# First norm's rows read from DMA instead of row products, and the experts' places put in a written order with one place more

## The chip, the cores and the metric

One NeuronCore of one Trainium2 chip runs the whole program. The metric is the device time of one execution in microseconds (us). The kernel before takes 1349.5 us, the median of 3 runs (1349.09 to 1349.57).

## The reference

Input `x` is 256 tokens by 1024. Everything is float32. Four layers follow each other; each is a mixer and then a mixture of experts.

```
h = layer_norm(x, ln0_g, ln0_b)
for i in 0, 1:                         # layers 0 and 1 of the kernel
    u   = h @ w_in[i]                  # 1024 x 2560; hyena, differential attention, pooling
    h   = layer_norm(a*h + concat(mixers(u)) @ w_out[i], ...)
    h   = layer_norm(a*h + moe16(h) + sigmoid(h @ ple_wg + b) * (p @ ple_wp), ...)
for i in 0, 1:                         # layers 2 (gmlp) and 3 (mla) of the kernel
    x   = x + concat(mixer_i(rms_norm(x)), memory_attention) @ w_out
    x   = x + moe32(rms_norm(x), ...)
# moe16: 4 groups x 4 experts; moe32: 4 groups x 8 experts; each token picks 2 experts of one group
# an expert: (silu(t @ w_gate) * (t @ w_up) * weight) @ w_down, with 1024x256, 1024x256, 256x1024 matrices
```

An expert has three matrices of 1 MiB each. The 32 experts of layer 2, and those of layer 3, are 96 MiB a layer and all of it is read once from HBM.

## The kernel before

**Dense part.** A weight matrix comes in units of 128 x 2048 numbers (1 MiB, two DMAs) into 4 raw slots of SBUF, issued by SP (line 585). ACT copies each half of a unit into `w_hi` (L1960, a rounded form), DVE subtracts it into `w_lo` (L2575), and PE does three products for one (L973 to L975). Activations are transposed on PE (L990) and split in the same way by ACT into `t_hi` (L1966) and by DVE into `t_lo` (L2587). `w_hi` and `w_lo` have 3 parts each.

**First norm.** SP loads `x` (L746), then one row of gains and one of biases, 4 KB each, into partition 0 (L748), then the first `w_in` units. Four PE products of a column of ones with a half row (`first_row`, L1447) spread the rows over 128 partitions in PSUM banks 0 to 3. DVE's `first_norm` (L3216) waits for them one after the other: `shift` (L2631) and `scale` (L2637) of the first half of the channels, `h_a`, then of the second half, `h_b`. The small constants come by a DMA that POOL issues.

**Experts of layers 2 and 3** (`slot_experts`). The work goes in steps of 4 experts (`ST_` = 4): 8 steps here. A step uses 12 transfers of 1 MiB in this order: 4 gates, 4 ups, 4 downs. I number the transfers of a layer from 0; group g is the transfers 4g to 4g+3, so groups 0, 1, 2 are gate, up and down of step 0, group 3 the gates of step 1, and so on. PE does gate and up with L1343 (64 products a group) and down with L1360 (32 products). Step 0 runs: the first gather of tokens (L1303, L1304, after DVE's `sel`), gate, `rows` (L1323 to L1326), up, `turn_glu` (L1351), down, then the second gather (16 products of each kind of 512 columns), and step 1 begins.

A transfer needs a place of 8 KB on each partition. The places are what the dense part leaves: 4 raw slots and 3 parts of `w_hi` and of `w_lo` (a0 to a9 in what follows), one that was `y` (OWN, a10), the region of `t_hi`/`t_lo` (FIRST_TOKENS, TOKENS, MORE_TOKENS: the gathered tokens take it back later), ROWS (the gain rows' buffer), SPARE, LATER, and in layer 3 MEMORY. The class `Ring` (L105) makes the list `units`, the place of each transfer: 12 of step 0, 12 of step 1, then `fixed` for all later steps. A transfer into a place that was used before waits on SP until the PE products that read it have counted up `used` (`ring.before`); a transfer into a fresh place waits for what the dense part had there (L714 to L733). SP issues in order (`ring.issued`), so a transfer that waits holds up all behind it. Fresh places: 16 in layer 2, 17 in layer 3. The list before, layer 2, with groups separated by bars:

```
step 0: ROWS SPARE LATER a0 | a1 a2 a3 a4 | a5 TOKENS MORE_TOKENS a6
step 1: a7 a8 a9 a10 | a0 a1 a2 a3 | a4 a5 a6 a7
later:  a8 a9 a10 a0 | a1 a2 a3 FIRST_TOKENS | a4 a5 a6 a7
layer 3, step 0: MEMORY ROWS SPARE LATER | a0 a1 a2 a3 | a4 a5 TOKENS MORE_TOKENS
layer 3, step 1: a6 a7 a8 a9 | a10 a0 a1 a2 | a3 a4 a5 a6
```

**Experts of layers 0 and 1** (`pair_experts`, `PairRing`). Steps of 2 experts with 6 transfers (2 gates, 2 ups, 2 downs; L642 and L646 issue them, L1123 and L1140 use them). The first two transfers go to the places SUMS and MEMORY, which come free before the ring's own places.

**DVE's selection** (`pick`, L3072): for each of two blocks of 128 tokens a `tensor_scalar` and a `scalar_tensor_tensor` write the gather's selection matrix; each waits for the one before it. It is used once for the first gather (`sel`), once for the second (`sel2`), and in the last steps (`select`).

Of the kernel before, what the change touches and what calls it, by code (L numbers as in the profile page):

```python
# [95 lines left out]
SUMS = LATER + 1  # L96
# [8 lines left out]
class Ring:  # L105


    MAIN = 6

    def __init__(self, unit, more, by_release):  # L110
# [9 lines left out]
        self.more = more  # L120
        first = more + a[0:6] + [TOKENS, MORE_TOKENS] + a[6:n]
        self.units = first + (a + a)[n:n + 12] + self.fixed * (self.MAIN - 2)
        fresh, release = range(13 + len(more)), by_release(a)
        self.issued = sorted(fresh, key=lambda i: release.index(self.units[i])) + [*range(len(fresh), self.MAIN * self.per)]

    def landed(self, n):
        for together in (self.more, [TOKENS, MORE_TOKENS]):
            if self.units[n] in together:
                return 16 * len(together)
        return 16 * self.units[0:n + 1].count(self.units[n])  # L130
# [20 lines left out]
class PairRing:  # L151
# [4 lines left out]
    def __init__(self, unit):  # L156
# [4 lines left out]
        self.units = [SUMS, MEMORY] + [r[n % 10] for n in range(self.main - 2)]  # L161
# [80 lines left out]
def program(nc, A, seen):  # L242

    ctx = ExitStack()
    with ctx:
# [117 lines left out]
        def place(slot):  # L363
            return {MEMORY: MEMW, SPARE: SPAREW, LATER: LATERW, SUMS: SUMSW}[slot] if slot > ROWS else EX[:, slot, :]

# [150 lines left out]
        class SlotSignals:  # L516
            def __init__(self, L):
# [32 lines left out]

        def ring_of(L, s):
            m = slot_signals[L]
            if m.ring is None:
                if L < DEPTH:
                    m.ring = PairRing(s.unit)
                elif L == 2:
                    m.ring = Ring(s.unit, [ROWS, SPARE, LATER], lambda a: [ROWS, OWN, SPARE, a[0], LATER] + a[1:10] +
                                  [TOKENS, MORE_TOKENS])
                else:
                    m.ring = Ring(s.unit, [MEMORY, ROWS, SPARE, LATER], lambda a: [MEMORY, a[0], a[1], OWN, a[2], ROWS, SPARE, LATER] +  # L560
                                  a[3:10] + [TOKENS, MORE_TOKENS])
# [12 lines left out]
        def _(sp):  # L574
# [61 lines left out]
            def load_pairs(L):  # L636
# [11 lines left out]
                n = 0  # L648
                for step in range(ring.STEPS):
                    for k in range(4 if step == 0 else 6):  # L650
                        slot, before = ring.units[n], ring.before(n)
                        if before is not None:
                            sp.wait_ge(m.used, before + 1)
                        elif slot in (SUMS, MEMORY):
                            sp.wait_ge(*turn_lo.at((("cat", L), 1)))
                        elif slot < RING:
                            sp.wait_ge(split_half[1], s.count(last_dense(s.unit, slot) + 1 - s.unit))
                        else:
                            sp.wait_ge(unit_used, s.count(last_dense(s.unit, slot) + 1 - s.unit))
                        if k < 4:  # L660
# [3211 lines left out]
```

## Time and profile before

| | |
|---|---|
| median of 3 runs | 1349.5 us |
| the profiled execution, its own time | 1349.16 us |
| span of its trace (first to last instruction) | 1345.9 us |
| PE busy | 1153.6 us (86%) |
| DVE busy | 704.4 us (52%) |
| ACT busy | 464.8 us (35%) |
| moved by DMA | 399.58 MB, mean 297 GB/s |

The profile page gives, for one execution, how long each engine was busy and what moved in 40 equal slices of the span. The chain that ended last is followed back from the last instruction to what released each step of it. Busy shares are averages over stages with different limits, so the stages have to be read one by one: where an engine waits, for whom, and whether DMA is moving data at that time. Between the profiled time and the span lie 3.3 us of start and end.

### The profile page before, as it was taken

What the parts mean: (1) busy time and instruction counts of PE and PEld (TensorE: products, weight loads), DVE (VectorE), ACT (ScalarE), POOL (GpSimd) and SP (SyncE); (2) the same over time, 40 slices, a digit from 0 to 9 for tenths busy, and PEclk for the clock granted to TensorE, in tenths of its full rate; (3) what the DMA queues carried; (4) which work ended last, traced back from release to release, by engine and by line L of the source; (5) the groups of instructions that cost most, each with busy time, mean ns of one, the idle gap of its engine ahead of it and who ended that gap; (6) DMA issues with size and microseconds to landing.
All of it is one profiled execution on the core that took longest, in us unless ns stands there. A gap on an engine that the chain in (4) does not pass through costs nothing.

```text
span 1345.9 us, 20019 instructions
## 1 busy us (share of the span) xinstructions
PE 1153.6 (86%) x7730; PEld 807.1 (60%) x7730; DVE 704.4 (52%) x1530; ACT 464.8 (35%) x863; POOL 166.3 (12%) x264
## 2 busy tenths in 40 slices
PE   7999999979999999989998966667799988755675
PEld 4888775547987765567876532334489775422342
DVE  6787854348778844376755521102477766211022
ACT  3574521125555322146743300000378643000010
POOL 4012200022030900011004000000222120000000
PEclk9999999989999999989998987878999998877888
DMA  9445489987346699975469699999843396899996
GB/s 329 150 157 173 159 356 422 390 320 233 126 136 234 224 404 420 401 260 168 159 227 373 235 414 421 421 420 422 333 168 125 126 373 270 354 421 421 421 420 287
DMA packets 94156, 399.58 MB, mean 297 GB/s; under 512 B 12124, under 2 KB 20060, under 8 KB 56948
## 3 DMA queue, kind: packets, MB, share of 16 engines
q1 hardware_dynamic: 84708, 381.98, 72.7%
q0 software_dynamic: 9360, 16.40, 3.9%
q8 instruction: 58, 0.95, 0.3%
q14 instruction: 30, 0.25, 0.1%
HBM read 397.29 MB, written 1.05 MB: 296 GB/s over the span
## 4 chain that ended last, share of the span: by engine, by line
PE 58%; DMA 23%; DVE 13%; ACT 4%; issue 2%; SPq 1%; DVEq 0%; ACTq 0%; POOLq 0%
DMA experts_at<-in_moe_w_down_dram 12%; DMA experts_at<-in_moe_w_up_dram 8%; PE bank L973 8%; PE bank L974 8%; PE bank L975 7%; PE bank L1123 7%; PE bank L1343 4%; PE bank L1360 4%; PE bank L1140 4%; DVE w_lo_at L2575 2%; PE bank L1150 2%; PE bank L990 1%; DMA experts_at<-in_moe_w_dram 1%; PE bank L1460 1%; PE bank L1303 1%
## 5 line engine op out<-in xcount | busy, mean ns | idle before, releaser
L973 PE MATMUL bank<-w_hi_at,t_hi_at 128*128 128x512 f32 (+3 forms) x528 | 209.7, 397 | 11.7 <-DVE t_lo_at L2597 4.1
L974 PE MATMUL bank<-w_lo_at,t_hi_at 128*128 128x512 f32 (+3 forms) x528 | 202.5, 383 | 0.0
L975 PE MATMUL bank<-w_hi_at,t_lo_at 128*128 128x512 f32 (+3 forms) x528 | 202.4, 383 | 0.0
L2575 DVE TENSOR_TENSOR w_lo_at<-raw_at,w_hi_at 128x1024 fp32r<-128x1024 f32 (+2 forms) x152 | 176.3, 1203 | 21.8 <-ACT w_hi_at L1960 16.3
L1960 ACT ACTIVATE w_hi_at<-raw_at 128x1024 fp32r<-128x1024 f32 (+2 forms) x152 | 148.8, 1035 | 35.0 <-PE bank L975 23.6
L1343 PE MATMUL bank<-experts_at,xs_at 128*32 128x256 f32 x1456 | 110.0, 454 | 51.4 <-DMA experts_at<-in_moe_w_gate_dram 32.7
L973 PEld LDWEIGHTS bank<-w_hi_at,t_hi_at 128*128 128x128 f32 x528 | 101.1, 192 | 36.0 <-issue 8.8
L1343 PEld LDWEIGHTS bank<-experts_at,xs_at 128*32 128x32 f32 x1456 | 61.7, 130 | 99.5 <-issue 82.6
L975 PEld LDWEIGHTS bank<-w_hi_at,t_lo_at 128*128 128x128 f32 x528 | 101.2, 192 | 18.9
L3153 DVE SCALAR_TENSOR_TENSOR glu_at<-silu_at,gate_at,bank 128x256 f32<-128x256 f32 x16 | 10.5, 657 | 194.7 <-ACT silu_at L2140 194.7
L974 PEld LDWEIGHTS bank<-w_lo_at,t_hi_at 128*128 128x128 f32 x528 | 101.4, 192 | 16.9 <-issue 0.5
L1360 PE MATMUL bank<-experts_at,act_t_at 128*32 128x512 f32 x512 | 78.6, 769 | 37.7 <-DMA experts_at<-in_moe_w_down_dram 35.3
L1123 PE MATMUL bank<-experts_at,xs_f_at 128*64 128x256 f32 x960 | 108.4, 380 | 0.0
L1123 PEld LDWEIGHTS bank<-experts_at,xs_f_at 128*64 128x64 f32 x960 | 69.5, 137 | 38.5 <-issue 8.6
L2140 ACT ACTIVATE silu_at<-bank,root_slot_at 128x256 f32<-128x256 f32 x16 | 7.6, 474 | 233.2 <-PE bank L1343 233.2
L3162 DVE TENSOR_TENSOR ys_lo_at<-bank,ys_hi_at 128x512 fp32r<-128x512 f32 x32 | 22.1, 691 | 106.0 <-ACT ys_hi_at L2153 105.9
L1360 PEld LDWEIGHTS bank<-experts_at,act_t_at 128*32 128x32 f32 x512 | 21.7, 136 | 85.9 <-issue 85.9
L1140 PE MATMUL bank<-experts_at,act_t_at 128*64 128x512 f32 x256 | 58.0, 595 | 0.2 <-DMA experts_at<-in_moe_w_dram 0.2
L2153 ACT ACTIVATE ys_hi_at<-bank 128x512 fp32r<-128x512 f32 x32 | 19.1, 598 | 108.9 <-PE bank L1360 108.9
L1343 PE MATMUL bank<-experts_at,xs_loop_at 128*32 128x256 f32 x512 | 40.0, 474 | 18.0 <-DMA experts_at<-in_moe_w_up_dram 12.4
L1343 PEld LDWEIGHTS bank<-experts_at,xs_loop_at 128*32 128x32 f32 x512 | 18.8, 135 | 36.7 <-issue 14.5
L2912 DVE TENSOR_TENSOR ys_lo_at<-bank,ys_hi_at 128x512 fp32r<-128x512 f32 x32 | 22.1, 691 | 34.9 <-ACT ys_hi_at L2047 34.5
(656 smaller groups left out, 2042.4 us busy)
## 6 DMA issues: line engine op xcount, KB each, us to landing
experts_at<-in_moe_w_dram SPq DMA_DIRECT2D x92, 1024.0 KB, 11.0
experts_at<-in_moe_w_up_dram SPq DMA_DIRECT2D x64, 1024.0 KB, 18.6
experts_at<-in_moe_w_down_dram SPq DMA_DIRECT2D x64, 1024.0 KB, 18.8
experts_at<-in_moe_w_gate_dram SPq DMA_DIRECT2D x59, 1024.0 KB, 18.1
raw_at<-in_w_in_dram SPq DMA_DIRECT2D x40, 512.0 KB, 6.3
raw_at<-in_a_w_in_dram SPq DMA_DIRECT2D x20, 512.0 KB, 4.6
raw_at<-in_w_out_dram SPq DMA_DIRECT2D x16, 512.0 KB, 4.2
raw_at<-in_ple_wg_dram SPq DMA_DIRECT2D x16, 512.0 KB, 5.1
```

The costliest lines, as they stand in the source:

```text
L973: pe.matmul(out, ah, bh, start=start, stop=False, skip_group_check=loose)
L974: pe.matmul(out, ah, bl, start=False, stop=False, skip_group_check=loose)
L975: return pe.matmul(out, al, bh, start=False, stop=stop, skip_group_check=loose)
L1123: ins = pe.matmul(out[C * t:C * t + C], x[:, j, off + C * t:off + C * t + C], w, start=first and n == 0, stop=last and n == len(chunks) - ...
L1140: ins = pe.matmul(BK[4 + half][C * t:C * t + C, :], ATF[:, i, C * t:C * t + C], place(slots[t])[:, a:a + 512], start=i == 0, stop=i == 1, ...
L1150: ins = pe.matmul(BK[2 * tb + half][:, :], st[:, tb * P:(tb + 1) * P], y[:, half * 512:half * 512 + 512], start=first and y is YHF, stop=F ...
L1343: ins = pe.matmul(out[C * t:C * t + C], x[:, j, off + C * t:off + C * t + C], w, start=first and n == 0, stop=last and n == len(chunks) - ...
L1360: ins = pe.matmul(BK[4 + half][C * t:C * t + C, :], ATT[:, i, C * t:C * t + C], place(slots[t])[:, a:a + 512], start=i == 0, stop=i == 1, ...
L1960: act.activation(WH[:, s.part(), a], RAW[:, s.slot(), a], ACT.Copy).then_inc(hi_half[i], 1)
L2575: dve.tensor_tensor(WL[:, s.part(), a], RAW[:, s.slot(), a], WH[:, s.part(), a].bitcast(F32), ALU.subtract).then_inc(split_half[i], 1)
L2912: dve.tensor_tensor(YLF[:, a], BK[4 + half][:, :], YHF[:, a].bitcast(F32), ALU.subtract)\
L3162: dve.tensor_tensor(YL2[:, a], BK[4 + half][:, :], YH2[:, a].bitcast(F32), ALU.subtract)\
```

## The change

- The two rows of the first norm are loaded by SP's DMA into all 128 partitions (512 KB each where 4 KB were), in front of the first `w_in` units. The four `first_row` products are gone; two products of 512 columns on constants stand on PE after the wait for the constants. DVE waits for both rows at once.
- `Ring` takes a plan: the lists of places for step 0, step 1 and later steps are written out for each layer. There is one place more, SUMS2, in the 8 KB where `x_t` lay (free when the router's logits are done), so 17 fresh places in layer 2 and 18 in layer 3. FIRST_TOKENS isn't used any more; SPARE (layer 2) and MEMORY (layer 3) stay in the later steps. `diag2` moves to another address. Which landing semaphores are shared changes with it.
- `PairRing` keeps its order of issue, but the transfers to SUMS and MEMORY are now the two ups of step 0, and the gates go to the ring's first two places.
- POOL loads the memory tokens of layer 1 after 4 uses rather than 2, and layer 3's gain rows (into ROWS) after 9 uses rather than 1.
- `pick` does the first operation for both blocks, one wait, the second for both, one wait; PE waits for one `sel` signal rather than two.

```
step 0, layer 2: SPARE LATER a0 a1 | a2 a3 a4 SUMS2 | ROWS TOKENS MORE_TOKENS a5
step 1, layer 2: a6 a7 a8 a9 | a10 SPARE a0 a1 | a2 a3 a4 a5          later: the same
step 0, layer 3: MEMORY SPARE LATER a0 | ROWS a1 a2 SUMS2 | a3 a4 TOKENS MORE_TOKENS
step 1, layer 3: a5 a6 a7 a8 | a9 a10 MEMORY SPARE | a0 ROWS a1 a2
later,  layer 3: a3 a4 a5 a6 | a7 a8 a9 a10 | MEMORY a0 a1 a2
```

```diff
-    def __init__(self, unit, more, by_release):
+    def __init__(self, unit, plan):
...
-        n = 10 - len(more)
-        b = (a + a)[n + 1:n + 12]
-        self.fixed = b[0:7] + [FIRST_TOKENS] + b[7:11]
+        first, second, self.fixed, release, self.together = plan(a)
...
-        first = more + a[0:6] + [TOKENS, MORE_TOKENS] + a[6:n]
-        self.units = first + (a + a)[n:n + 12] + self.fixed * (self.MAIN - 2)
-        fresh, release = range(13 + len(more)), by_release(a)
+        self.units = first + second + self.fixed * (self.MAIN - 2)
+        fresh = range(len(release))
...
-        self.units = [SUMS, MEMORY] + [r[n % 10] for n in range(self.main - 2)]
+        self.units = r[0:2] + [SUMS, MEMORY] + [r[n % 10] for n in range(2, self.main - 2)]
+        self.issued = [2, 3, 0, 1] + [*range(4, self.main)]
...
-        DG2, XT = sb("diag2", [P, 10, P], z.at), sb("x_t", [P, DC, T], z.at)
+        XT, SUMS2W = sb("x_t", [P, DC, T], z.at), sb("sums_place2", [P, UNIT], z.at)
         YH2, YL2 = (z.take(n, [P, D], F32R) for n in ("ys_hi2", "ys_lo2"))
         SEL = z.take("sel2", [P, TB, 512], F32R)
+        DG2 = sb("diag2", [P, 10, P], z.at)
...
+        def gmlp_places(a):
+            turns = a[6:11] + [SPARE] + a[0:6]
+            return ([SPARE, LATER] + a[0:5] + [SUMS2, ROWS, TOKENS, MORE_TOKENS, a[5]], turns, turns,
+                    [ROWS, OWN, SPARE, a[0], LATER] + a[1:10] + [TOKENS, MORE_TOKENS, SUMS2], (ROWS, TOKENS, MORE_TOKENS))
+
+        def mla_places(a):
+            return ([MEMORY, SPARE, LATER, a[0], ROWS, a[1], a[2], SUMS2, a[3], a[4], TOKENS, MORE_TOKENS],
+                    a[5:11] + [MEMORY, SPARE, a[0], ROWS, a[1], a[2]], a[3:11] + [MEMORY] + a[0:3],
+                    [MEMORY, a[0], a[1], OWN, a[2], ROWS, SPARE, LATER] + a[3:10] + [TOKENS, MORE_TOKENS, SUMS2],
+                    (TOKENS, MORE_TOKENS))
...
+                    elif slot == SUMS2:
+                        sp.wait_ge(*small_ready.at(("logits_t", L)))
...
-                    elif slot == FIRST_TOKENS:
-                        sp.wait_ge(m.used, per + 2 * G)
...
-                sp.dma_start(ROW[0:1, slot, :], A[n].rearrange("(a n) -> a n", a=1)).then_inc(*first_rows.tick("ln0"))
+                sp.dma_start(ROW[:, slot, :], A[n].partition_broadcast(P)).then_inc(*first_rows.tick("ln0"))
...
-                    pool.wait_ge(slot_signals[L].used, 2)
+                    pool.wait_ge(slot_signals[L].used, 4)
...
-                        (A["b_kn_g_2"][0][P:192], 0, 832)], (slot_signals[2].used, 1))
+                        (A["b_kn_g_2"][0][P:192], 0, 832)], (slot_signals[2].used, 9))
...
-            pe.wait_ge(*first_rows.at("ln0"))
-
-            def first_row(half, slot):
-                pe.matmul(BK[2 * half + slot][:, :], ONES[0:1, :], ROW[0:1, slot, 512 * half:512 * half + 512],
-                          start=True, stop=True).then_inc(*small_ready.tick(("ln0_row", half, slot)))
-            first_row(0, 0)
-            first_row(0, 1)
...
+            for _ in range(2):
+                pe.matmul(BK[7][:, :], IDENT, CS[:, 0:512], start=True, stop=True)
...
-                def pick(c, tb, key, a, ramp, sel=SEL):
-                    c.do(dve.tensor_scalar(sel[:, tb, a], ramp, key[:, 0, tb:tb + 1], None, ALU.is_equal))
-                    c.do(dve.scalar_tensor_tensor(sel[:, tb, a], ramp, key[:, 1, tb:tb + 1], sel[:, tb, a].bitcast(F32),
-                                                  ALU.is_equal, ALU.add))
+                def pick(c, key, a, ramp, sel=SEL):
+                    for tb in range(TB):
+                        c.go(dve.tensor_scalar(sel[:, tb, a], ramp, key[:, 0, tb:tb + 1], None, ALU.is_equal))
+                    c.sync()
+                    for tb in range(TB):
+                        c.go(dve.scalar_tensor_tensor(sel[:, tb, a], ramp, key[:, 1, tb:tb + 1], sel[:, tb, a].bitcast(F32),
+                                                      ALU.is_equal, ALU.add))
+                    c.sync()
...
-                dve.wait_ge(*small_ready.at(("ln0_row", 0, 0)))
-                shift(X, 0, row_in_bank)
+                dve.wait_ge(*first_rows.at("ln0"))
+                shift(X, 0, row_of)
                 rooted("ln0", TB)
-                dve.wait_ge(*small_ready.at(("ln0_row", 0, 1)))
-                scale(X, 0, row_in_bank)
+                scale(X, 0, row_of)
```

## Rows read from the trace of the kernel before

**Rows 1.** The page, its chain that ended last: shares of the span by engine.
```profile
PE 58%; DMA 23%; DVE 13%; ACT 4%; issue 2%; SPq 1%; DVEq 0%; ACTq 0%; POOLq 0%
```

**Rows 2.** By stretch, layers 2 and 3: length, busy per engine, granted PEclk, DMA share, GB/s.
```profile
741.00:747.00 6.00, 6.00 (x85) 4.25 (x84) 5.46 (x23) 2.47 (x6) 0.15 (x1) 1.00 0.00 0
...
769.00:774.00 5.00, 5.00 (x71) 3.10 (x71) 2.88 (x10) 0.00 (x0) 0.00 (x0) 1.00 0.13 16
774.00:958.00 184.00, 121.68 (x1162) 61.48 (x1160) 31.92 (x84) 15.47 (x34) 0.00 (x0) 0.83 1.01 419
...
1121.00:1130.00 9.00, 7.50 (x112) 4.93 (x104) 5.53 (x17) 2.67 (x5) 0.00 (x0) 1.00 0.05 8
...
1146.00:1150.00 4.00, 4.00 (x55) 2.55 (x48) 1.89 (x7) 0.00 (x0) 0.00 (x0) 1.00 0.23 31
1150.00:1334.00 184.00, 121.17 (x1161) 62.18 (x1159) 31.91 (x84) 15.47 (x34) 0.00 (x0) 0.83 1.00 416
```

**Rows 3.** Instructions in time, PE, layer 2: start us, us, what, [idle before, releaser].
```profile
769.07 3.66 PE L1343 MATMUL bank<-experts_at,xs_at 128*32 128x256 f32 x64
...
781.06 3.64 PE L1360 MATMUL bank<-experts_at,act_t_at 128*32 128x512 f32 x32 [0.56 <-ACT act_t_at L2144]
788.97 6.21 PE L1343 MATMUL bank<-experts_at,xs_at 128*32 128x256 f32 x64 [4.27 <-DMA experts_at<-in_moe_w_gate_dram]
```

**Rows 4.** The same view, SP's DMA issues, layer 2.
```profile
746.71 7.17 SPq L697 DMA_DIRECT2D experts_at<-in_moe_w_up_dram  x4
...
772.74 0.33 SPq L701 DMA_DIRECT2D experts_at<-in_moe_w_down_dram  x1
```

**Rows 5.** The same view, SP's DMA issues, layer 3.
```profile
1128.51 0.33 SPq L697 DMA_DIRECT2D experts_at<-in_moe_w_up_dram  x1
...
1148.58 0.33 SPq L701 DMA_DIRECT2D experts_at<-in_moe_w_down_dram  x1
```

**Rows 6.** The same view, PE, layer 3: up of step 0, gate of step 2.
```profile
1124.83 3.66 PE L1343 MATMUL bank<-experts_at,xs_at 128*32 128x256 f32 x64
...
1164.49 1.94 PE L1343 MATMUL bank<-experts_at,xs_at 128*32 128x256 f32 x16 [4.23 <-DMA experts_at<-in_moe_w_gate_dram]
```

**Rows 7.** The same view, DVE, layer 2: a block's selection, and a pair without a wait.
```profile
737.29 0.36 DVE L3073 TENSOR_SCALAR sel_at<-ramp_at,keys_at 128x256 fp32r<-128x256 f32 x1 [0.18 <-DVE sel_at L3074]
...
744.69 0.28 DVE L3109 TENSOR_SCALAR diag_at<-consts_at,w_at 128x128 f32<-128x128 f32 x1
744.88 0.48 DVE L3111 TENSOR_SCALAR diag_at<-consts_at,rs_at 128x128 f32<-128x128 f32 x2
```

**Rows 8.** The same view, the first 18 us, four engines' rows.
```profile
9.24 1.41 DVE L2631 SCALAR_TENSOR_TENSOR x_at<-x_at,mv_at,bank 128x512 f32<-128x512 f32 x2 [1.78 <-PE bank L1447]
...
11.11 2.01 ACT L1960 ACTIVATE w_hi_at<-raw_at 128x1024 fp32r<-128x1024 f32 x2 [3.36 <-DMA raw_at<-in_w_in_dram]
...
13.70 0.60 ACT L1966 ACTIVATE t_hi_at<-bank 128x512 fp32r<-128x512 f32 x1 [0.58 <-PE bank L990]
...
15.12 1.28 DVE L2587 TENSOR_TENSOR t_lo_at<-bank,t_hi_at 128x512 fp32r<-128x512 f32 x2
...
17.49 0.79 PE L973 MATMUL bank<-w_hi_at,t_hi_at 128*128 128x512 f32 x1
```

**Rows 9.** Layer 0: SP's issue in time, and a stretch (columns as Rows 2).
```profile
183.24 0.82 SPq L642 DMA_DIRECT2D experts_at<-in_moe_w_dram  x2
...
196.00:200.00 4.00, 4.00 (x37) 2.50 (x36) 2.27 (x6) 0.47 (x2) 0.00 (x0) 1.00 0.15 64
```

**Rows 10.** In time: layer 3's first loads, and ACT's use of their second and third unit.
```profile
945.40 11.63 SPq L585 DMA_DIRECT2D raw_at<-in_b_w_in_dram  x8
...
968.14 3.28 ACT L1960 ACTIVATE w_hi_at<-raw_at 128x640 fp32r<-128x640 f32 x4
```

**Rows 11.** In time: POOL's loads of memory tokens (layer 1) and of gain rows (layer 2).
```profile
469.84 1.06 POOL L783 DMA_DIRECT2D mem_at<-in_mem_dram  x2
...
746.85 0.54 POOL L772 DMA_DIRECT2D row_at<-in_b_kv_norm_g_dram  x1 [7.75 <-PE bank L1343]
```

More of the change, by code:

```diff
@@ L95 @@
 FIRST_TOKENS, TOKENS, MORE_TOKENS, ROWS, MEMORY, SPARE, LATER = OWN + 1, OWN + 2, OWN + 3, OWN + 4, OWN + 5, OWN + 6, OWN + 7
-SUMS = LATER + 1
+SUMS, SUMS2 = LATER + 1, LATER + 2
 def last_dense(unit, slot):
@@ L363, in place @@
         def place(slot):
-            return {MEMORY: MEMW, SPARE: SPAREW, LATER: LATERW, SUMS: SUMSW}[slot] if slot > ROWS else EX[:, slot, :]
+            return {MEMORY: MEMW, SPARE: SPAREW, LATER: LATERW, SUMS: SUMSW, SUMS2: SUMS2W}[slot] if slot > ROWS else EX[:, slot, :]
         z = Space(z_at, z_size)
@@ L523, in __init__ @@
                 else:
-                    once = {slot: "once" if slot >= ROWS else "tokens" for slot in range(TOKENS, LATER + 1)}
-                    self.land = [sem(f"s{L}_land_{once.get(slot, slot)}") for slot in range(LATER + 1)]
+                    self.land = {}
                 self.used = sem(f"s{L}_used")
@@ L553, in ring_of @@
             if m.ring is None:
[L554 to L561, printed above, removed]
+                m.ring = PairRing(s.unit) if L < DEPTH else Ring(s.unit, gmlp_places if L == 2 else mla_places)
+                if L >= DEPTH:
+                    for slot in m.ring.units:
+                        name = "together" if slot in m.ring.together else slot
+                        m.land[slot] = sem(f"s{L}_land_{name}")
             assert m.ring.unit == s.unit, (L, m.ring.unit, s.unit)
@@ L646, in down @@
                     sp.dma_start(place(slot)[:, :], src).then_inc(m.land[ring.pair[slot]], 16)
[L648 to L660, printed above, removed]
-                            up(slot, 2 * step + k % 2, k // 2)
-                        else:
-                            down(slot, 2 * step - 2 + k % 2)
-                        n += 1
+                steps = [(0, k) for k in range(4)] + [(step, k) for step in range(1, ring.STEPS) for k in range(6)]
+                for n in ring.issued:
+                    step, k = steps[n]
+                    slot, before = ring.units[n], ring.before(n)
+                    if before is not None:
+                        sp.wait_ge(m.used, before + 1)
+                    elif slot in (SUMS, MEMORY):
+                        sp.wait_ge(*turn_lo.at((("cat", L), 1)))
+                    elif slot < RING:
+                        sp.wait_ge(split_half[1], s.count(last_dense(s.unit, slot) + 1 - s.unit))
+                    else:
+                        sp.wait_ge(unit_used, s.count(last_dense(s.unit, slot) + 1 - s.unit))
+                    if k < 4:
+                        up(slot, 2 * step + k % 2, k // 2)
+                    else:
+                        down(slot, 2 * step - 2 + k % 2)
                 sp.wait_ge(*dve_ready.at(("table", L)))
@@ L1314, in slot_experts @@
                 pe.wait_ge(*pool_ready.at(("hl", L, 1)))
-                for tb in range(TB):
-                    pe.wait_ge(*dve_ready.at(("sel", L, tb)))
+                pe.wait_ge(*dve_ready.at(("sel", L)))
                 first_gather(range(5))
@@ L2623, in row_of @@
                 return ROW[:, slot, 512 * half:512 * half + 512]
-            def row_in_bank(slot, half):
-                return BK[2 * half + slot][:, :]
             def shift(buf, half, row):
@@ L3114, in slot_experts @@
                 dve.wait_ge(*gathered.at((L, DC - 1)))
-                for tb in range(TB):
-                    pick(ch, tb, KLS, slice(0, 512), RAMP[:, :])
+                pick(ch, KLS, slice(0, 512), RAMP[:, :])
                 done(("sel2", L))
@@ L3120, in select @@
                 def select(c):
-                    for tb in range(TB):
-                        pick(c, tb, KLS, slice(0, P), IOTA, SELL)
+                    pick(c, KLS, slice(0, P), IOTA, SELL)
                     dve.nop().then_inc(*m.sel.tick())
@@ L3232, in first_norm @@
                 sync()
-                dve.wait_ge(*small_ready.at(("ln0_row", 1, 1)))
-                scale(X, 1, row_in_bank)
+                scale(X, 1, row_of)
                 done(("h_b", 0))
```

21 lines of the change are left out of this document (6 added, 15 removed).

## The prediction

> **What bounds the kernel now.** I began with the chain that ended last: PE carries 58% of it, DMA 23%, DVE 13% [rows 1]. The kernel therefore has two kinds of stage, and an edit has to be priced in its own. The table by stretch separates them [rows 2]. In layer 2 from 774 to 958 and in layer 3 from 1150 to 1334 the DMA share is 1.0 at 419 and 416 GB/s, while PE works 122 and 121 of 184 us: there only bytes count. Just ahead of both stretches DMA stands nearly still: 0 GB/s in 741 to 747, 16 in 769 to 774, 8 in 1121 to 1130, 31 in 1146 to 1150, with PE busy nearly throughout. PE, running step 0, sets that time.
>
> Why DMA stands still is read from SP. In layer 2 it issues when a group of PE products has freed places: at 746.71 (end of gate 0) and at 772.74 (end of gate 1, which began at 769.07 and took 3.66) [rows 3, 4]. Layer 3 does the same at 1128.51, the end of up 0, and 1148.58, the end of gate 1 [rows 5, 6]. No place is free in between. Later PE waits: gate 2 begins at 788.97 after 4.27 us of waiting for DMA, in layer 3 at 1164.49 after 4.23 [rows 3, 6].
>
> So the end of each layer is the moment at which transfers stop being held up (after gate 1) plus the transfers left then. One is 1.0486 MB; at 419 GB/s it takes 2.50 us, at 416 2.52. From 774 to 958 that is 184/2.50 = 73.5, and 96 less the 23 moved before is 73: the picture closes. **A transfer moved earlier, into the idle time, is worth 2.5 us.**
>
> **The change part by part.**
>
> *Places.* I counted both lists of places by hand: how many transfers, in order of issue, have a place at the start and after gate 0, up 0, down 0 and gate 1 (later groups in the same way).
>
> Layer 2, before: 16, 17, 21, 23, 27. After: 17, 20, 23, 24, 28.
> Layer 3, before: 17, 17, 21, 23, 27. After: 18, 21, 24, 26, 30.
>
> What counts is the column after down 0, since these can have landed when gate 1 ends. Layer 2 goes from 23 to 24: only the extra place counts. Layer 3 goes from 23 to 26: the extra place, and two that came back late before, because MEMORY and two of its neighbours in step 0 weren't in the later steps or were followed in the list by places freed only by an up or a down.
>
> Is there room? In layer 2, SUMS2 (free with the router's logits, ahead of the first gather) lands inside the idle 741 to 747. The three of 746.7 take 7.5 us and end near 754, the three after up 0 (near 752.5) near 762, the one after down 0 (near 761.6) near 765; the loads for the new row at POOL add about 1 us, and gate 1 ends only at 772.7. In layer 3, the three after gate 0 (near 1123) end near 1131, three after up 0 (1128.5) near 1138.6, two after down 0 near 1143.6; gate 1 ends at 1148.5. All fits, with 5 us or more to spare. Afterwards both rings turn with the same 12 transfers a step, and PE has 62 us of slack in 184, so the lead isn't lost. Gain: 1 x 2.50 in layer 2, 3 x 2.50 = 7.5 in layer 3; together 10.0. Lead above zero can't turn into a loss by itself, but SUMS2 can be late: in layer 3 it is issued a little before 1121 and lands by 1123.6 to 1124, up 0 begins at 1124.83 [rows 6]. The margin is some 0.5 us or more; I take 0, with a bound of 1 us lost.
>
> Against that sum a page can be held: the Trainium skill, DMA: Bandwidth & Descriptors, section Where 436 GB/s comes from, says that for transfers from HBM a core's share of some 358 GB/s binds. By it, as an estimate, a transfer would take 2.93 us and the ten would be 11.7. The trace has 419 and 416 GB/s [rows 2], and the measurement decides.
>
> *Selection.* `pick` stands on the way to the first gather, when DMA is idle, so what it saves moves all of gate 0 to gate 1, the whole rest of the layer with it. Now each of the four operations waits for the one before (0.18 us idle ahead of one [rows 7]). Two waits go. An operation of 128 columns takes 0.28, and two in a row without a wait take 0.48 together, not 0.56 [rows 7]: an overlap of 0.08. Each pair gains 0.18 - 0.04 (the gap that remains, by the nearest such rows) + 0.04 to 0.08, about 0.18; two pairs 0.37, both layers 0.74. `sel2` and `select` get it too, but PE doesn't wait for them. Bounds 0 and 1.0.
>
> The rule against it: the Trainium skill, VectorE: DVE Perf Modes, section The DRAIN you can't avoid, says that dropping semaphores between VectorE operations gains nothing, the next one starts when the pipe is empty either way. By it this term is 0; the trace has the overlap of 0.08 for the pair at 744.88.
>
> *First norm.* The rows bring 1 MB ahead of the first `w_in` unit, 2.50 us at 419 GB/s. Before, `shift` began at 9.24, after 1.78 us of waiting for a row product, and ACT began on the first unit at 11.11, waiting for DMA [rows 8]. After: the rows stand behind `x`, whose statistics DVE has before its wait begins at 7.46; 1.25 us for each of the two puts them near 8.5 (an estimate), so `shift` gains up to 0.7; ACT begins at 11.11 + 2.5 = 13.6, `w_hi` takes 2.01 to 15.6, two `t_hi` of 0.60 to 16.9, and the second `t_lo` (half of 1.28) to 17.5. The first unit's products began at 17.49 [rows 8]: the loss on DMA is met by slack, since `t_hi` waited for PE before (0.58 ahead of 13.70), where row products stood in front of the transposes. I take 0. If ACT's delay counted in full it is +2.6; if the four products in front of the unit were what held it, -1.0.
>
> *Layers 0 and 1.* SP's issue for the gates no longer stands behind SUMS and MEMORY's, which wait for the split at 183.24; but DMA is saturated there until 196 and then idles at 64 GB/s until PE releases places [rows 9]. PE bounds the stage: 0, bounds -0.5 and +0.5.
>
> *Order of the other queues.* Layer 3's first raw units (SP, 945.40 [rows 10]) go into places that the last downs now free, some 5 us later; ACT's need of the second and third unit is at 968.14, and they land near 963.5 and 966: hidden, by 0 to 1 us lost. POOL's memory tokens wait for 4 uses, which are there at about 470, when POOL now gets to them (469.84); the gain rows wait for 9 uses and so come near 761 rather than 746.85 [rows 11]; behind them on POOL stands nothing that is needed before layer 3's norms: 0. The two products on constants at the start lie ahead of the wait for `x`: 0.
>
> **Sum:** -10.0 - 0.74 + 0 = -10.7. Against the profiled 1349.16 this is 1338.4; the median of the runs is 0.3 above the profiled one, so 1338.8.
>
> **Rivals.**
> 1. Only the extra place counts and layer 3's new order is absorbed: the ups that stand early in the list wait for places of another group and the lead at gate 1 is 1, as in layer 2. Gain 2.5 + 2.5 + 0.7: 1343.8. For it: some place in the list may be held by more than my count of uses. Against: SP's issue times before fit the count exactly [rows 4, 5]. 0.15.
> 2. The start is late in full (+2.6): 1341.4. For it: ACT waits for DMA there [rows 8]. 0.07.
> 3. The page's rule on waits holds for the pair with `is_equal`: no gain in `pick`, 1338.8 + 0.74 = 1339.5. 0.10.
> 4. The places don't do what the list says, because a common landing signal makes a down wait for a place that lands later, or because the lead is given back in the later steps: 1348.8 with the selection alone. 0.05.
> 5. Slower: TensorE's clock. In 741 to 747 PE is granted 1.00 with DMA idle; under saturation it is 0.83 [rows 2], and a group of 64 products takes 6.21 rather than 3.66 (factor 1.70) [rows 3]. Now transfers run beside step 0. If it ran at the lower of the two levels (1.2 GHz for 2.4), gather, gate, rows and up, some 14.3 us a layer, would cost 0.70 x 14.3 = 10 more; over both layers 20 - 10.7 = 9.3, 1358.8. It decides from where about 15 us of step 0 run at the lower level. Against: gate 1 still takes 3.66 right before saturation, and PE has no gap in which it would sink. 0.04.
>
> **How the numbers follow.** Forecast 1338.8 with 0.59; its own range 1336.5 to 1341.5, from the bounds (-1.0 to +2.6 at the start, 1 for SUMS2, 0.5 to 1 elsewhere, which don't meet at once). Rivals 2 and 3 lie in it. Up to rival 1 the range is 1336.5 to 1344.0. A measurement tells 0.2% (2.7 us) from no change; 1346.8 is the border. Faster: forecast and rivals 1 to 3, 0.91; same: rival 4, 0.05; slower: rival 5, 0.04.
>
> **What would show it.** In layer 2 and layer 3 SP issues three transfers at the end of gate 0; the stall ahead of gate 2 falls from 4.27 to 1.5 in layer 2 and to nothing in layer 3; saturation ends near 955 and 1323.5; first unit's products near 17.5 and ACT's first `w_hi` near 13.6; PE waits under 0.5 us for SUMS2. Wrong would be an idle DMA after 774, gate 0 or up 0 over 3.7 us, or a first unit after 18.5.

## The result, and the profile after

The changed kernel takes 1338.8 us (median of 6 runs, 1337.4 to 1342.6) where the kernel before takes 1349.05 beside it. The ratio is 0.9930, 95% interval 0.9914 to 0.9947: 9.4 us faster, 7.2 to 11.6. The forecast was 1338.8. The profiled execution is the longest of the six (1342.6, span 1340.6), so I read it mark by mark and don't take its sum. One execution of a kernel below, the one with layer 3's old places, took 1428.6 at a granted clock of 0.81; it is left out, and that kernel's median is of its other 11.

The table by stretch, columns as in [rows 2]:

```profile
741.00:747.00 6.00, 6.00 (x85) 4.25 (x85) 5.50 (x23) 1.80 (x4) 0.00 (x0) 1.00 0.09 16
...
769.00:774.00 5.00, 5.00 (x71) 2.89 (x70) 2.88 (x10) 0.52 (x1) 0.00 (x0) 1.00 0.00 0
774.00:958.00 184.00, 125.87 (x1172) 65.09 (x1174) 31.39 (x84) 15.44 (x34) 0.00 (x0) 0.81 1.01 417
1121.00:1130.00 9.00, 8.53 (x132) 5.54 (x124) 6.23 (x22) 1.64 (x4) 0.00 (x0) 1.00 0.67 262
1146.00:1150.00 4.00, 4.00 (x67) 2.34 (x67) 2.88 (x10) 0.00 (x0) 0.00 (x0) 1.00 0.10 39
1150.00:1334.00 184.00, 125.38 (x1201) 65.34 (x1200) 32.08 (x85) 16.44 (x36) 0.00 (x0) 0.83 0.97 400
```

In layer 3 the nine microseconds from 1121, idle before (8 GB/s), now move 262 GB/s. Saturation then ends before 1334, which is why that stretch shows 400 and not 416. DMA still stands still from 769 to 774, so the idle time isn't used up.

SP's issues answer to [rows 4, 5]. Three transfers are now issued at the end of gate 0 in both layers, where there were one and none. In the last line below one transfer belongs to the end of gate 0, and three to the end of up 0, from 1129.5 on.

```profile
745.91 0.33 SPq L702 DMA_DIRECT2D spare_place_at<-in_moe_w_up_dram  x1
746.28 0.91 SPq L702 DMA_DIRECT2D experts_at<-in_moe_w_up_dram  x2
...
1123.52 0.33 SPq L702 DMA_DIRECT2D memory_place_at<-in_moe_w_up_dram  x1
1123.89 0.43 SPq L702 DMA_DIRECT2D spare_place_at<-in_moe_w_up_dram  x1
1124.37 6.45 SPq L706 DMA_DIRECT2D experts_at<-in_moe_w_down_dram  x4
```

PE, against [rows 3, 6]: gate 2 follows down 1 with no wait in both layers, where 4.27 and 4.23 us were. The wait comes one group later, at up 2, 4.25 us in layer 2 and 2.28 in layer 3. In layer 2 this trace flatters the change: part of down 1 ran at the lower clock and took 5.34 us, not 3.64. In the five other kernels with 24 transfers by the end of down 0 whose down 1 took 3.64 (e2, e3, e4, g3, h1), gate 2 still waits 1.7 to 1.9 us.

```profile
781.62 5.34 PE L1364 MATMUL bank<-experts_at,act_t_at 128*32 128x512 f32 x32 [0.57 <-ACT act_t_at L2137]
786.96 3.66 PE L1347 MATMUL bank<-experts_at,xs_at 128*32 128x256 f32 x64
...
796.90 0.60 PE L1347 MATMUL bank<-experts_at,xs_at 128*32 128x256 f32 x1 [4.25 <-DMA experts_at<-in_moe_w_up_dram]
...
1161.13 3.66 PE L1347 MATMUL bank<-experts_at,xs_at 128*32 128x256 f32 x64
1169.11 3.66 PE L1347 MATMUL bank<-experts_at,xs_at 128*32 128x256 f32 x64 [2.28 <-DMA experts_at<-in_moe_w_up_dram]
```

The start, against [rows 8]: `shift` waits 4.44 us for the biases and begins at 12.02 instead of 9.24, ACT gets its first unit at 15.54 instead of 11.11, the first products come at 19.41 instead of 17.49.

```profile
12.02 1.41 DVE L2621 SCALAR_TENSOR_TENSOR x_at<-x_at,mv_at,row_at 128x512 f32<-128x512 f32 x2 [4.44 <-DMA row_at<-in_ln_b_dram]
...
15.54 2.00 ACT L1953 ACTIVATE w_hi_at<-raw_at 128x1024 fp32r<-128x1024 f32 x2 [7.67 <-DMA raw_at<-in_w_in_dram]
...
19.41 0.79 PE L978 MATMUL bank<-w_hi_at,t_hi_at 128*128 128x512 f32 x1 [1.33 <-DVE t_lo_at L2580]
```

**One table for all runs.** Whole times of single executions differ by several us. The distances between fixed events of PE differ less, so every trace was read at the same marks (us). A: start of the first product of the first unit. B: from the start of the last product on the one-hots (the router's choices, L1296 before) to the start of layer 2's first gather; layer 3's behind it. C: from the end of gate 1 to the start of up 2. D: from the end of gate 1 to the end of the layer's last down. E: from layer 3's first unit to its first gather.

| kernel | median | A | B | C, layer 2 | C, layer 3 | D, layer 2 | D, layer 3 | E |
|---|---|---|---|---|---|---|---|---|
| before | 1349.05 | 17.5 | 4.12, 4.11 | 26.2 | 26.3 | 189.0 | 189.6 | 145.3 |
| before, 2nd trace (f5) | 1351.3 (one) | 17.5 | 4.13, 4.00 | 25.9 | 26.6 | 189.1 | 190.2 | 149.3 |
| changed | 1338.8 | 19.4 | 3.81, 3.72 | 23.6 | 19.5 | 188.1 | 183.8 | 146.5 |
| changed, again (e1) | 1338.95 | 19.1 | 3.73, 3.71 | 23.5 | 18.6 | 188.0 | 181.6 | 146.4 |
| first norm of before (e2) | 1336.9 | 17.4 | 3.62, 3.60 | 23.8 | 18.8 | 186.5 | 181.6 | 147.6 |
| no extra place (e3) | 1339.7 | 19.4 | 3.60, 3.60 | 23.7 | 18.7 | 186.6 | 181.5 | 147.7 |
| layer 3's old places (e4) | 1346.1 | 19.3 | 3.61, 3.61 | 23.8 | 26.2 | 186.7 | 190.2 | 147.6 |
| layer 2's old places (f8) | 1342.65 | 18.9 | 3.61, 3.72 | 26.4 | 19.4 | 190.5 | 183.9 | 146.5 |
| ROWS twice (f6) | 1340.3 | 18.5 | 3.61, 3.61 | 23.5 | 18.9 | 187.2 | 181.7 | 146.1 |
| ROWS twice, old first norm (f7) | 1339.6 | 17.5 | 3.63, 3.72 | 23.8 | 18.6 | 187.2 | 181.5 | 146.5 |
| ROWS twice, gain rows late (g1) | 1339.1 | 18.9 | 3.74, 3.71 | 21.3 | 18.7 | 184.3 | 181.6 | 146.7 |
| the same, old first norm (g2) | 1334.3 | 17.9 | 3.72, 3.61 | 21.3 | 19.6 | 184.2 | 182.7 | 146.3 |
| old selection (g3) | 1340.1 | 18.9 | 4.00, 4.12 | 23.6 | 19.1 | 186.7 | 183.0 | 147.3 |
| pair ring of before (h1) | 1340.3 | 18.5 | 3.61, 3.61 | 23.8 | 19.5 | 186.7 | 183.6 | 147.7 |

### The profile page after: what moved, and what is told of

The parts are those of the page before. It is cut to its first block, busy times and chain, and to the rows that moved or that the text cites. A ratio compares the mean times of both kernels' runs of the same rounds, so it can differ in the third digit from the quotient of the medians.

```text
span 1340.6 us, 19996 instructions
## 1 busy us (share of the span) xinstructions
PE 1153.4 (86%) x7726; PEld 810.8 (60%) x7726; DVE 703.0 (52%) x1530; ACT 464.0 (35%) x863; POOL 164.4 (12%) x264
## 4 chain that ended last, share of the span: by engine, by line
PE 55%; DMA 24%; DVE 13%; ACT 4%; issue 2%; SPq 2%; DVEq 0%; ACTq 0%
DMA experts_at<-in_moe_w_down_dram 20%; PE bank L978 8%; PE bank L980 8%; PE bank L979 8%; PE bank L1364 6%; PE bank L1128 6%; PE bank L1145 4%; DMA experts_at<-in_moe_w_dram 4%; DVE w_lo_at L2568 2%; PE bank L1347 2%; PE bank L1155 1%; PE bank L1457 1%; PE bank L995 1%; SPq L706 1%; PE bank L1308 1%
## 5 line engine op out<-in xcount | busy, mean ns | idle before, releaser
L980 PEld LDWEIGHTS bank<-w_hi_at,t_lo_at 128*128 128x128 f32 x528 | 102.0, 193 | 19.1
L1364 PE MATMUL bank<-experts_at,act_t_at 128*32 128x512 f32 x464 | 82.9, 807 | 17.9 <-DMA experts_at<-in_moe_w_down_dram 15.7
L2146 ACT ACTIVATE ys_hi_at<-bank 128x512 fp32r<-128x512 f32 x32 | 19.1, 597 | 111.7 <-PE bank L1364 111.7
L1364 PE MATMUL bank<-memory_place_at,act_t_at 128*32 128x512 f32 x48 | 30.9, 806 | 18.1 <-DMA experts_at<-in_moe_w_down_dram 18.1
L2902 DVE TENSOR_TENSOR ys_lo_at<-bank,ys_hi_at 128x512 fp32r<-128x512 f32 x32 | 22.1, 692 | 34.9 <-ACT ys_hi_at L2040 34.5
## 6 DMA issues: line engine op xcount, KB each, us to landing
experts_at<-in_moe_w_gate_dram SPq DMA_DIRECT2D x59, 1024.0 KB, 17.9
experts_at<-in_moe_w_up_dram SPq DMA_DIRECT2D x53, 1024.0 KB, 18.6
```

What stands on the lines that cost most here:

```text
L980: return pe.matmul(out, al, bh, start=False, stop=stop, skip_group_check=loose)
L1364: ins = pe.matmul(BK[4 + half][C * t:C * t + C, :], ATT[:, i, C * t:C * t + C], place(slots[t])[:, a:a + 512], start=i == 0, stop=i == 1, ...
L2146: act.activation(YH2[:, half * 512:half * 512 + 512], BK[4 + half][:, :], ACT.Copy).then_inc(*m.yh.tick())
L2902: dve.tensor_tensor(YLF[:, a], BK[4 + half][:, :], YHF[:, a].bitcast(F32), ALU.subtract)\
```

## The experiments

**The changed kernel again** (e1).

> The changed kernel once more, for a second profile beside the others and a closer median. My account: 1338.8 give or take 1, with 1.4 to 1.9 us lost at the start, about 2 won by layer 2's places and 7 by layer 3's. If the profiled execution shown so far (1342.6, where its other runs lie between 1337.4 and 1341.5) was long by a disturbance, the new profile shows where: I expect the difference at the end of layer 3 and in layer 2's step 0, where PE's granted clock was lower, not in the start. If both profiles have the same places, the spread is elsewhere.

1338.95 (1337.6 to 1341.9), ratio 0.9926 [0.9907, 0.9944]. The account of the marks holds. Column D of layer 3 was 2.2 us longer in the first trace of the changed kernel than here, with the same places and issues; in layer 2 both are 1.5 us longer than the variants e2 to e4. In all these cases a stretch at the lower of the two clocks (half-clock stretch in what follows) fell on the last down. It took 5.04 and 5.08 us in layer 2 of the two traces, against 3.64 in e2 to e4, and in layer 3 5.06 in the first trace, against 3.64 here. Layer 2's, first in the changed kernel, then in e2:

```profile
956.40 5.04 PE L1364 MATMUL bank<-experts_at,act_t_at 128*32 128x512 f32 x32 [2.96 <-DMA experts_at<-in_moe_w_down_dram]
```
```profile
953.16 3.64 PE L1364 MATMUL bank<-experts_at,act_t_at 128*32 128x512 f32 x32 [0.32 <-DMA experts_at<-in_moe_w_down_dram]
```

So 1 to 2 us of an execution hang on where such a stretch falls, and C is the safer reading of a lead than D. Two traces don't tell whether the place in layer 2 is this kernel's or chance.

**The first norm of before** (e2), in the changed kernel:

```diff
-                sp.dma_start(ROW[:, slot, :], A[n].partition_broadcast(P)).then_inc(*first_rows.tick("ln0"))
+                sp.dma_start(ROW[0:1, slot, :], A[n].rearrange("(a n) -> a n", a=1)).then_inc(*first_rows.tick("ln0"))
... and the four first_row products with their waits again, without the two products on constants
```

> The changed kernel with the first norm of before (rows of 4 KB and row products). If the rows' load costs at the start what the trace shows, shift at 12.0 rather than 9.2, this kernel is 1.4 to 1.9 us faster than the changed one, near 1337.2, and its first unit's products begin near 17.5. If the loss at the start is given back later, both are the same within 0.4. If the rows' load were a gain hidden by something else, this one is slower.

1336.9, 2.1 less than the changed kernel on the same chip; the first products are at 17.43 again, `shift` at 9.19, and the SP queue's first unit reaches ACT at 11.16:

```profile
9.19 1.41 DVE L2635 SCALAR_TENSOR_TENSOR x_at<-x_at,mv_at,bank 128x512 f32<-128x512 f32 x2 [1.62 <-PE bank L1451]
...
11.16 2.00 ACT L1964 ACTIVATE w_hi_at<-raw_at 128x1024 fp32r<-128x1024 f32 x2 [3.31 <-DMA raw_at<-in_w_in_dram]
```

The spreads of the two kernels overlap (1335.1 to 1342.0 and 1337.6 to 1341.9), so the time alone would not settle it; the mark A does. This part of the change costs 1.0 to 1.9 us by A. In the three pairs of kernels that differ in it alone, the old first norm is faster each time, by 2.1 (e1, e2), 0.7 (f6, f7) and 4.8 us (g1, g2). That nothing gives it back later is likely by that, but not shown: the way from A to layer 2's first gather varies from 716.8 to 722.0 us between traces.

**No extra place** (e3).

```diff
-            turns = a[6:11] + [SPARE] + a[0:6]
-            return ([SPARE, LATER] + a[0:5] + [SUMS2, ROWS, TOKENS, MORE_TOKENS, a[5]], turns, turns,
+            turns = a[7:11] + [SPARE] + a[0:7]
+            return ([SPARE, LATER] + a[0:6] + [ROWS, TOKENS, MORE_TOKENS, a[6]], turns, turns,
... and the same in layer 3
```

> The changed kernel without the place SUMS2: 16 fresh places in layer 2, 17 in layer 3, 11 and 12 free ones to turn with, lists otherwise in the new order. My count (transfers that can be issued when down 0 ends): one fewer in each layer, so 2 x 2.5 = 5.0 us slower than the changed kernel, near 1343.8. The rival, that the order alone brings the gain and the 17th place is idle, gives the same time as the changed kernel. The other rival, that the place in layer 3 makes up 0 wait, gives a gain in layer 3.

1339.7, and C is 23.7 and 18.7, just what the changed kernel has. The expectation of 5 us failed. Its reason, that the extra place is what counts, was an inference I had never counted through. Counted, this kernel's list gives 24 and 26 transfers after down 0, the same as with the place, and that is what C shows. Down 1 took 3.64 us here, so that gate 2 does wait, 1.82 us:

```profile
786.00 3.66 PE L1347 MATMUL bank<-experts_at,xs_at 128*32 128x256 f32 x64 [1.82 <-DMA experts_at<-in_moe_w_gate_dram]
795.93 0.38 PE L1347 MATMUL bank<-spare_place_at,xs_at 128*32 128x256 f32 x1 [4.23 <-DMA experts_at<-in_moe_w_up_dram]
```

**Layer 3's places of before** (e4).

```diff
         def mla_places(a):
+            return old_places(a, [MEMORY, ROWS, SPARE, LATER], ...)     # the list of before, FIRST_TOKENS in it
```

> The changed kernel with layer 3's places of before (17 fresh, FIRST_TOKENS in the later steps, every place with a landing signal of its own). My count: three transfers fewer moved when gate 1 of layer 3 ends, so 7.5 us slower than the changed kernel, near 1346.3. The rival that only the extra place counts in layer 3 gives 2.5, near 1341.3.

1346.1, 7.2 us more than the changed kernel on the same chip (7.5 expected; by their ratios to the kernel before, 0.9973 and 0.9926, it is 6.3), and C of layer 3 is back at 26.2, with the wait ahead of gate 2:

```profile
1165.32 6.21 PE L1353 MATMUL bank<-experts_at,xs_at 128*32 128x256 f32 x64 [4.09 <-DMA experts_at<-in_moe_w_gate_dram]
```

Two thirds to three quarters of the whole gain are layer 3's list.

**The kernel before again** (f5).

> The kernel before, unchanged, for a second profile. The trace of before has no half-clock stretch in the first units of layer 3 (966 to 975), the four traces of the new kernel's variants have one there of 3.4 us, and lose 1.1 to 2.3 us between layer 3's first unit and its first gather. Theory one, the place of the half-clock stretches is a matter of each execution: this profile has its own places, and the time between these two marks (145.3 in the first profile) can come out near 147. Theory two, the later loads of layer 3's raw units cause it: 145.3 again.

E is 149.3, against 145.3 in its first trace. That speaks for theory one: the half-clock stretches take their own places in each execution. The granted clock of a stretch is the mean over it. The stretch from 966 to 975, first in the second trace of before (granted 0.62), then in the changed kernel (0.81); the first trace of before had 1.00:

```profile
966.00:975.00 9.00, 6.77 (x28) 6.71 (x28) 7.54 (x13) 4.49 (x9) 8.07 (x13) 0.62 0.66 204
```
```profile
966.00:975.00 9.00, 6.76 (x38) 6.53 (x37) 8.28 (x14) 5.66 (x11) 8.15 (x11) 0.81 0.85 281
```

Had I had one trace of before only, the 1.1 to 2.3 us that all variants lose in E would have been put down to layer 3's later raw units. An effect of those by a microsecond isn't excluded by E.

**ROWS used twice in layer 2** (f6), one transfer more by the count:

```diff
-            return ([SPARE, LATER] + a[0:5] + [SUMS2, ROWS, TOKENS, MORE_TOKENS, a[5]], turns, turns,
+            return ([SPARE, ROWS, LATER] + a[0:4] + [SUMS2, a[4], TOKENS, MORE_TOKENS, a[5]],
+                    a[6:11] + [SPARE, ROWS] + a[0:5], a[5:11] + [SPARE] + a[0:5],
...
-                        (A["b_kn_g_2"][0][P:192], 0, 832)], (slot_signals[2].used, 9))
+                        (A["b_kn_g_2"][0][P:192], 0, 832)], (slot_signals[2].used, 19))
```

> The changed kernel, with ROWS used twice in layer 2 (in gate 0 and in up 1; the gain rows are loaded after 19 uses). By my count 25 rather than 24 transfers can be issued when down 0 ends, so one transfer more has moved when gate 1 ends: 2.5 us faster than the changed kernel, near 1336.4, and up 2 begins 21.1 us after gate 1's end rather than 23.6. The rival, that the lead at that point is set by DMA and not by places: no difference, 1338.9. If the gain rows at POOL come too late for layer 3: over 1 us slower there.

1340.3, and C of layer 2 is 23.5: no gain, although gate 2 came without a wait 11.8 us after gate 1 rather than 13.7. The trace shows why. Layer 3's gain rows, which need the same buffer, left the idle time (762 in the changed kernel) and went into the saturated one:

```profile
776.66 0.54 POOL L777 DMA_DIRECT2D row_at<-in_b_kv_norm_g_dram  x1 [38.29 <-PE bank L1347]
...
782.43 3.66 PE L1347 MATMUL bank<-experts_at,xs_at 128*32 128x256 f32 x64
...
794.13 0.64 PE L1347 MATMUL bank<-experts_at,xs_at 128*32 128x256 f32 x2 [5.99 <-DMA experts_at<-in_moe_w_up_dram]
```
```profile
774.00:780.00 6.00, 3.73 (x58) 1.81 (x54) 2.57 (x7) 0.86 (x2) 2.13 (x4) 1.00 1.01 422
780.00:787.00 7.00, 7.00 (x96) 4.01 (x88) 2.88 (x9) 1.20 (x2) 0.00 (x0) 1.00 0.99 318
787.00:800.00 13.00, 6.99 (x69) 3.60 (x68) 0.00 (x0) 0.00 (x0) 0.00 (x0) 0.74 1.01 423
```

Seven microseconds at 318 instead of 422 GB/s with the DMA share at 0.99: 0.7 MB not moved, and 0.46 MB of what was moved are the rows themselves. Together 1.2 MB or 2.8 us of the experts' transfers, one transfer's worth.

**ROWS twice, in the kernel with the old first norm** (f7).

> Both edits together: ROWS used twice in layer 2, and the first norm of before. 2.5 and 2.0 us add: 1334.4 from 1338.9. If one hides the other, 1336.5.

1339.6 (1334.3 to 1342.9), C 23.8: the same in the kernel with the old first norm, the transfer isn't won. The expected 1334.4 was missed by 5.2 us. 2.5 of them are that transfer; the other 2.7, by which it is slower than e2 at the same C, no mark explains, and they lie within what its executions differ by.

**The gain rows late** (g1), which tests that reading:

```diff
-                        (A["b_kn_g_2"][0][P:192], 0, 832)], (slot_signals[2].used, 19))
+                        (A["b_kn_g_2"][0][P:192], 0, 832)], dve_ready.at(("moe_out", 2)))
```

> The changed kernel with ROWS used twice in layer 2, and layer 3's gain rows loaded after layer 2's output instead of in its step 1. In the kernel that used ROWS twice alone, these 448 KB ran at 780 to 787 beside the experts' transfers: the SP queue moved 1.76 MB in 7 us where it moves 2.93, which is 2.8 us, as much as the transfer won (2.5). If that is why nothing was won, this kernel has the stretch at 420 GB/s, up 2 begins 21.1 us after gate 1's end rather than 23.5, layer 2's last down ends 184 us after it rather than 187.2, and the time is 1336.4. If places or PE bound instead, it stays at 1339 to 1340. If the rows come too late for layer 3's norm (needed 18 us after layer 2's output), the first gather of layer 3 comes later by what DVE waits.

C of layer 2 is 21.3 (21.1 expected), D 184.3 (184), 422 GB/s right after:

```profile
787.00:800.00 13.00, 10.85 (x136) 7.04 (x132) 1.09 (x2) 0.60 (x1) 0.00 (x0) 0.87 1.01 422
...
795.32 0.41 PE L1347 MATMUL bank<-experts_at,xs_at 128*32 128x256 f32 x2 [2.15 <-DMA experts_at<-in_moe_w_up_dram]
```

The time of 1339.1 doesn't show the 2.5 us (1337.8 to 1342.0; its ratio, 0.9919 [0.9902, 0.9935], against 0.9926 and 0.9930 of the changed kernel). By time alone this kernel is undecided; the marks are what shows the mechanism.

**The gain rows late, in the kernel with the old first norm** (g2).

> The same with the first norm of before: 2.0 us less, 1334.4, if the two add; 15 us less than the kernel before.

1334.3 (4 runs, 1333.7 to 1336.8), ratio 0.9878 [0.9859, 0.9898]: 16 us faster than the kernel before, and the best kernel found. It is what was expected, but not for the expected reason alone: it is 4.8 us faster than g1, and A gives 1.0 of them. The marks support 3.5 to 4 us against the changed kernel, one transfer and the first norm; the rest may be luck of four executions.

**Layer 2's places of before** (f8), in the changed kernel:

```diff
         def gmlp_places(a):
+            return old_places(a, [ROWS, SPARE, LATER], ...)
```

> The changed kernel with layer 2's places of before (16 fresh, 11 that come back in step 1 instead of 12). By count 23 rather than 24 at the end of down 0: 2.5 us slower than the changed kernel, 1341.4, and up 2 begins 26.2 us after gate 1's end rather than 23.6. The rival, that the gain in layer 2 is from other parts (selection, landing signals): no difference between these marks.

C is 26.4 (26.2 expected), 2.8 more than with the new list, with the old wait ahead of gate 2, here 4.49 us. The time is 1342.65 (1339.9 to 1349.5), 3.7 more than e1's on another chip, where 2.5 were expected. One transfer, one count.

**The selection of before** (g3), in the changed kernel:

> The changed kernel with the selection of before (a wait after each of the four operations, two signals). In the traces the first gather begins 4.12 and 4.11 us after the last product on the one-hots before, 3.81 and 3.72 with the change. My account: this kernel shows 4.1 in both layers and is 0.7 us slower than the changed one, which its time can hardly show but its trace can. The rival by the page's rule (dropped waits gain nothing): 3.8 and 3.7 here too.

B is 4.00 and 4.12 again, against 3.60 to 3.81 in every kernel with the new selection. The last product on the one-hots takes 0.26 us where the granted clock is 1.00 (here, layer 2) and 0.37 where it is 0.50 (before, layer 2). Counted from its end, the way is 3.73 to 3.75 with the old selection and 3.34 to 3.37 with the new (3.44 once): 0.4 saved in each layer. First the changed kernel's rows, then e1's, then this one's:

```profile
736.39 0.71 DVE L3064 TENSOR_SCALAR sel_at<-ramp_at,keys_at 128x256 fp32r<-128x256 f32 x2
737.14 0.88 DVE L3067 SCALAR_TENSOR_TENSOR sel_at<-ramp_at,keys_at,sel_at 128x256 fp32r<-128x256 f32 x2
```
```profile
737.60 0.63 DVE L3064 TENSOR_SCALAR sel_at<-ramp_at,keys_at 128x256 fp32r<-128x256 f32 x2
738.26 0.88 DVE L3067 SCALAR_TENSOR_TENSOR sel_at<-ramp_at,keys_at,sel_at 128x256 fp32r<-128x256 f32 x2
```
```profile
734.20 0.49 DVE L3065 SCALAR_TENSOR_TENSOR sel_at<-ramp_at,keys_at,sel_at 128x256 fp32r<-128x256 f32 x1
734.87 0.35 DVE L3064 TENSOR_SCALAR sel_at<-ramp_at,keys_at 128x256 fp32r<-128x256 f32 x1 [0.18 <-DVE sel_at L3065]
```

The time (1340.1, 1338.0 to 1344.3) can't show 0.7 us.

**The pair ring of before** (h1), in the changed kernel: its list, its order of issue and the memory tokens after 2 uses.

> The changed kernel with the pair ring of before (layers 0 and 1: the two gates of step 0 in SUMS and MEMORY, issued first) and the memory tokens after 2 uses. My account: these layers are bound by PE where the order changed, so the time is the changed kernel's, 1338.9 within the spread of executions, and from the first unit to layer 2's first gather it takes 717 to 722 us as in all others. If the new order brings the experts' start forward, this kernel is slower there by what the four transfers' earlier issue is worth, up to 2.5 us a layer.

1340.3 (1339.1 to 1344.1). From the first unit to layer 2's first gather it takes 718.7 us, the other traces 716.8 to 722.0, before 720.9 and 719.6. No effect is seen; one of up to 1 or 2 us in either direction isn't excluded.

## Why the prediction was right, and where it was not

**Places, layer 3: right in count, price and room.** Three transfers at 2.5 us, 7.5. Measured at C: 26.3 and 26.6 before, 18.6 to 19.6 after, 7.4 on average; by the time, 7.2 (e4), by the ratios 6.3. The idle room was there, and the lead was kept to the end: D is 8.0 shorter in the traces without a late half-clock stretch (189.6 to 181.6). Wrong was only that one of the three was put down to the extra place: without it C is 18.7 (e3).

**Places, layer 2: number right, reason wrong.** One transfer, 2.5; C says 2.6 (26.2 to 23.6), f8 2.8. The stall ahead of gate 2 was to fall to 1.5; 4.27 less 2.50 is 1.77, and 1.7 to 1.9 is what the traces with a down 1 of 3.64 us show. But the step said "only the extra place counts", and so did rival 1. Taking SUMS2 away changes nothing (e3). What sets the number after down 0 is 12 plus the places that come back in time for the first two steps: before 11 in both layers (FIRST_TOKENS comes in only with the later steps), after 12 in layer 2, where SPARE is used twice, and 14 in layer 3, where MEMORY, SPARE and ROWS are. A place that is used once, like SUMS2, has been counted out by then: it moves transfers forward within step 0, where there is room for them anyway. The count was in the prediction; I put a cause to it without counting the list that would have tested it. Ordered by the count after down 0, all traces give one line: C is 25.9 to 26.6 with 23 transfers, 23.5 to 23.8 with 24, 21.3 with 25 (g1, g2) and 18.6 to 19.6 with 26. Only f6 and f7 leave it, with 25 by the count and the gain rows in the way.

**SUMS2 late in layer 3: right, no wait.** Up 0 begins 2.35 us after gate 0's end before (1122.48 to 1124.83), and 2.36 after (1123.51 to 1125.87).

**Selection: size right, the parts of the sum not.** 0.37 a layer was said, 0.31 and 0.39 measured at B, 0.4 from the product's end. The sum took 0.18 of idle time ahead of each operation, from one row. In the traces the three gaps were 0.04, 0.18 and 0.04, and are 0.04 once now. So 0.22 of idle time went, not 0.28, and both pairs overlap by 0.08: two operations of 0.48 take 0.88, and the first two, of 0.35 or 0.37, take 0.61 to 0.64 (0.71 in one trace, where the first took 0.45). The Trainium skill, VectorE: DVE Perf Modes, section The DRAIN you can't avoid, measures eight copies that gain nothing by dropped semaphores, and adds that a next operation that is not held starts earlier. This pair goes by the addition and not by the copies: the next operation starts 0.08 us before the one in front of it ends, and g3 takes 0.4 us more than all kernels with the new selection.

**First norm: wrong.** I took 0 and it costs 1.9 in the first trace (A, 17.49 to 19.41), 2.1 by e2's time; inside the bound of 2.6, but past 18.5, which the prediction itself had named as a sign of being wrong. The step that failed is "1.25 us for each of the two puts them near 8.5". The rate of 419 GB/s is that of the saturated stretches; in the first 14 us all queues together moved 276 GB/s before and 257 after. The rows landed 8.2 and 9.9 us after their issue at 1.62 and 2.09, and the first unit reached ACT 4.43 us later than before (15.54), where 2.5 was said:

```profile
row_at<-in_ln_g_dram SPq DMA_DIRECT2D x1, 512.0 KB, 8.2
row_at<-in_ln_b_dram SPq DMA_DIRECT2D x1, 512.0 KB, 9.9
```

[rows 8] had the answer: the megabyte that stood in this very place, the first raw unit, reached ACT at 11.11. Rows put there would land near 11, not 8.5 (the second landed at 11.99), and `shift` would begin two us later than it did. Why the queue moves so little at the start (constants by POOL's DMA run beside it, in small pieces) wasn't tried.

**Layers 0 and 1, the other queues: 0, as said**, as far as it can be seen (h1). From layer 2's last down to layer 3's first unit it takes 7.56 to 7.59 us in all traces, before and after, and ACT begins the second unit 5.76 us after the first, before (962.38, 968.14) as after (962.07, 967.83), without a wait for DMA: the later raw units are hidden. Left out was a condition of the step on POOL's loads, that their DMA must also find an idle time: at 762 it did, at 777 (f6) it cost 2.8 us.

**The slower rival** (TensorE's clock in step 0): from layer 2's first gather to the end of gate 1 it takes 34.3 and 34.5 before, 35.0 and 34.8 in the two traces of the changed kernel, 33.4 to 34.0 in most variants, and gate 0 and up 0 take 3.66 us in all. Nothing of the 10 us a layer.

**The sum.** -7.4 (layer 3) - 2.6 (layer 2) - 0.7 (selection) + 1.9 (start) = -8.8; the ratio says -9.4. Layer 2's 2.6 is by C; D of the changed kernel's own two traces gives 1.0, because its last down took 1.4 longer. From the end of the last down to the end of the trace it takes 7.7 and 7.8 us before and 7.1 in the changed kernel; these 0.6 were in no sum, and their cause is open (7.1 in the variants too, 8.1 in g3). The forecast of -10.7 was 1.9 too good at the start. That it met the measured 1338.8 to the tenth is luck: six executions of this kernel lie 5 us apart, and the kernel before was 0.45 faster beside it than at the forecast.

## What to carry to other kernels

Where a stage is bound by transfers, find the moment at which they stop being held up and count, from the written lists, how many can be issued by then; each one more is worth its time, here 2.5 us, and a place that is used only once may be worth nothing, as here. Count every variant that the explanation speaks of, not only the two at hand. A transfer's price is that of its stretch: take the landing of what stood in the same place, not the rate of a saturated stage; and a small load moved out of an idle stretch into a full one costs more than its bytes.

## What the hardware showed beyond that

- 448 KB of gain rows spread over the partitions (POOL's queue) in a saturated stretch brought the total from 422 to 318 GB/s for 7 us with the DMA share at 0.99: 2.8 us for what would be 1.1 us by bytes.
- The same kernel's executions differ by 3 to 10 us (1337.4 to 1342.6 for the changed kernel), and half-clock stretches fall on other stages each time: the same nine us of the kernel before had a granted clock of 1.00 in one trace and 0.62 in the next (6.8 us of it at half clock, an estimate from the mean), and layer 3's dense part took 145.3 and 149.3 us.
